# HGRN and forgetting-attention decays computed beside the first projection, one fewer matmul per attention score tile, and idle bf16 matmuls around the HGRN stage

## The reference

```python
# layer 0 of first_block
proj = x @ ev_w_in[e]
qa, fa, ia, ga, qb, kb, vb, fb = split_cols(proj, [HALF] * 7 + [FOX_HEADS])
ya = hgrn2(qa, fa, ia, ga, lb_all[layer], ev_hgrn_norm_g[e])
yb = forgetting_attention(qb, kb, vb, fb, ev_fox_bf[e])
mix = jnp.concatenate([ya, yb], axis=-1) @ ev_w_out[e]
# hgrn2: 4 heads of 128; lb = softmax-cumsum of a small table
log_f = jnp.log(lb + (1.0 - lb) * jax.nn.sigmoid(z))
k = (1.0 - lb) * jax.nn.sigmoid(-z)
b = cumsum(log_f)                    # the decay exponent, over time
# scores from q*exp(b), k*exp(-b), state passed from block to block, rms norm over 128, gate
# forgetting_attention: 8 heads of 64
log_f = jax.nn.log_sigmoid(f_logit + b_f)
c = jnp.cumsum(log_f, axis=1)
logits = q @ k.T * scale + c[query] - c[key]     # then mask, softmax, @ v
```

## Time and profile before

| what | us |
|---|---|
| median of the three timed runs | 3848.94 |
| the profiled execution's own time | 3850.37 |
| its span | 3848.6 |
| TensorE busy in it | 3598.5 (94%) |
| VectorE, ScalarE, GpSimd busy | 1619.7, 1334.2, 552.4 |
| first projection, last matmul begins at | 178.12 |
| attention stage, first matmul begins at | 316.82 |

### The profile page before, as it was taken

One profiled execution on the slowest core, in us unless ns is written; L12 is line 12 of the kernel. 1 busy time (PEld: TensorE's weight loads), 2 busy tenths in 40 slices (PEclk: granted clock), 3 DMA queues, 4 the chain that ended last, 5 costly groups with the idle time before them and its releaser, 6 DMA issues. The chain is left out here.

```text
span 3848.6 us, 42102 instructions
## 1 busy us (share of the span) xinstructions
PE 3598.5 (94%) x15648; PEld 2825.8 (73%) x15662; DVE 1619.7 (42%) x2091; ACT 1334.2 (35%) x1864; POOL 552.4 (14%) x446
## 2 busy tenths in 40 slices
PE   8878999998889999899998889999999999789998
PEld 7675668886666888688885468887788875578885
DVE  2284443335554333433345743335333235743335
ACT  3232232224553222433232543324333233533324
POOL 0030121101022110221000012202221000022202
PEclk9985899999999999999999899999999999899999
DMA  4200123322112332233220023322233220123322
GB/s 136 81 1 1 44 71 98 107 85 67 49 44 77 98 107 79 77 94 108 82 91 34 13 83 96 106 97 75 90 96 108 84 79 28 33 82 94 109 81 72
DMA packets 77745, 294.18 MB, mean 76 GB/s; under 512 B 8624, under 2 KB 11184, under 8 KB 77360
## 3 DMA queue, kind: packets, MB, share of 16 engines
q1 hardware_dynamic: 77616, 292.45, 23.9%
HBM read 290.32 MB, written 2.10 MB: 76 GB/s over the span
## 5 line engine op out<-in xcount | busy, mean ns | idle before, releaser
L146 DVE TENSOR_TENSOR w_low<-w_raw,w_high 128x1024 fp32r<-128x1024 f32 (+4 forms) x513 | 672.7, 1311 | 1578.5 <-ACT w_high L141 1578.5
L180 PE MATMUL bank<-x_high,w_high 128*128 128x512 f32 x2856 | 1130.4, 396 | 74.5 <-POOL x_low L224 22.0
L181 PE MATMUL bank<-x_low,w_high 128*128 128x512 f32 x2856 | 1120.4, 392 | 0.0
L182 PE MATMUL bank<-x_high,w_low 128*128 128x512 f32 x2856 | 1120.3, 392 | 0.0
L141 ACT CAST w_high<-w_raw 128x1024 fp32r<-128x1024 f32 (+4 forms) x513 | 555.0, 1082 | 872.8 <-PE bank L182 867.1
L180 PEld LDWEIGHTS bank<-x_high,w_high 128*128 128x128 f32 x2856 | 541.0, 189 | 206.4 <-issue 38.2
L182 PEld LDWEIGHTS bank<-x_high,w_low 128*128 128x128 f32 x2856 | 541.1, 189 | 113.3
L181 PEld LDWEIGHTS bank<-x_low,w_high 128*128 128x128 f32 x2856 | 541.9, 190 | 112.0 <-issue 2.1
L182 PE MATMUL bank<-hidden_high,w_low 128*128 128x512 f32 x1056 | 411.4, 390 | 0.0
L180 PE MATMUL bank<-hidden_high,w_high 128*128 128x512 f32 x1056 | 411.4, 390 | 0.0
L181 PE MATMUL bank<-hidden_low,w_high 128*128 128x512 f32 x1056 | 411.4, 390 | 0.0
(11 more groups left out here) (481 smaller groups left out, 3799.9 us busy)
## 6 DMA issues: line engine op xcount, KB each, us to landing
w_raw<-in_stream SPq DMA_DIRECT2D x381, 512.0 KB, 3.5
w_raw<-in_stream SPq DMA_DIRECT2D x96, 704.0 KB, 4.0
w_raw<-in_stream SPq DMA_DIRECT2D x16, 384.0 KB, 3.1
dft_positions<-in_dft SPq DMA_DIRECT2D x2, 2048.0 KB, 7.4
w_raw<-in_stream SPq DMA_DIRECT2D x4, 576.0 KB, 3.7
h<-in_x SPq DMA_DIRECT2D x8, 256.0 KB, 6.0
w_raw<-in_stream SPq DMA_DIRECT2D x16, 128.0 KB, 2.1
out<-result SPq DMA_DIRECT2D x4, 512.0 KB, 2.6
```

What stands on the lines that cost most here:

```text
L146: self.nc.vector.tensor_tensor(self.lo[:, j % 2, 0:size], self.raw[:, j % RAW_SLOTS, 0:size], self.hi[:, j % 2, 0:size].bitcast(F32), ALU. ...
L180: nc.tensor.matmul(out, lhs[0], rhs[0], start=start, stop=False)
L181: nc.tensor.matmul(out, lhs[0], rhs[1], start=False, stop=False)
L182: return nc.tensor.matmul(out, lhs[1], rhs[0], start=False, stop=stop)
```

## The change

- A new class `DecaySide` takes over the whole preparation of the HGRN stage, the constants and the forgetting-attention decays, cut into pieces that `linear_block` calls behind given jobs of the first projection. `constants_stage` and `fox_decay_stage` are gone, and with them two barriers. The transfer of the level masks moves from the HGRN stage to the head of the projection's DMA list.
- The eight-row steps of the attention decay stand behind jobs 21 to 26, the 16 scans behind jobs 16 to 19, the small table behind jobs 0 to 2, the constants behind job 3, the affine steps behind jobs 8 and 13.
- c is kept in one tensor `fox_c_parts` of 72 rows (high part in rows 0 to 7, low part in 64 to 71, zeros between), so that one matmul with `ident_fox` adds both. It now comes first in a unit, then the mask, then q by k.
- TensorE gets 14 idle bf16 matmuls at the end of the first projection, 8 between the last head's output and its variance, and 24 behind that variance.

```diff
@@ linear_block, after all jobs
+            if side:
+                side.end_pe(nc, C, pe, S)
@@ hgrn_stage, TensorE
-                pe.wait_ge(S.dve_step, 2 + 2 + 5 + HALF_T)
...
                     mm.then_inc(S.o_done, 1)
+                keep_warm(nc, C, C.bank[0], 8)
                 variance(HALF_T - 1)
+                keep_warm(nc, C, C.bank[0], 24)
@@ new
+class DecaySide:
+    NEGATED, PLUS, LOGS, SCAN, FOX = 7, 12, 14, 16, 21
...
+    def on_sync(self, nc, C, sp, S):
+        sp.dma_start(self.masks[:, :, :], C.level_dram).then_inc(S.masks_in, 16)
...
+    def end_pe(self, nc, C, pe, S):
+        pe.wait_ge(S.masks_in, 16)
+        pe.wait_ge(S.set, 9)
+        pe.wait_ge(S.evacuated, 4 + 21)
+        keep_warm(nc, C, C.bank[0], 14)
+
+    def on_act(self, nc, C, act, S, j):
...
+        if j == self.NEGATED:
+            act.wait_ge(S.evacuated, 4 + 8)
+            nc.scalar.activation(self.kk[:, :, :], prj[:, 4:8, :], ACT.Sigmoid,
+                                 scale=-1.0).then_inc(S.negated, 1)
+        if j == self.PLUS:
+            act.wait_ge(S.negated, 1)
+            nc.scalar.activation(prj[:, 4:8, :], prj[:, 4:8, :], ACT.Sigmoid).then_inc(S.plus, 1)
+        if j == self.LOGS:
+            act.wait_ge(S.f_ready, HALF_T)
+            nc.scalar.activation(prj[:, 4:8, :], prj[:, 4:8, :], ACT.Ln).then_inc(S.logs_ready, 1)
...
+    def on_dve(self, nc, C, dve, S, j):
...
+        if self.SCAN <= j < self.SCAN + HALF_T:
+            dve.wait_ge(S.logs_ready, 1)
+            for c in range(NB):
...
@@ scores
-                nc.tensor.matmul(bank[:, 0:keys], prj[r, 12 + t, qb * P:(qb + 1) * P],
-                                 prj[r, 16 + t, 0:keys], start=True, stop=False)
-                for part in (c_hi, c_lo):
-                    nc.tensor.matmul(bank[:, 0:keys], C.pick(h), part[:, 0:keys], start=False, stop=False)
-                return nc.tensor.matmul(bank[:, qb * P:keys], C.ident_bf, C.mask_after,
-                                        start=False, stop=True)
+            nc.tensor.matmul(bank[:, 0:keys], C.pick_fox(h), c_parts[:, 0:keys], start=True, stop=False)
+            nc.tensor.matmul(bank[:, qb * P:keys], C.ident_bf, C.mask_after, start=False, stop=False)
+            return nc.tensor.matmul(bank[:, 0:keys], prj[r, 12 + t, qb * P:(qb + 1) * P],
+                                    prj[r, 16 + t, 0:keys], start=False, stop=True)
```

More of the change, by code:

```diff
@@ L1397, in _, with hgrn_stage @@
                                                 ALU.mult).then_inc(S.normed, 1)
-def hgrn_stage(nc, C, prj, kk, va):
+def hgrn_stage(nc, C, prj, kk, va, masks):
     with ExitStack() as ctx:
@@ L1432, in hgrn_stage @@
         NL = LEVELS + 2
-        with stage(nc, "fetched act_step dve_step lb_in lb_exp f_ready logs_ready b_ready diff_ready decay_ready "
-                       "k_ready q_ready level_done masked_ready level_used turned copied state_done "
+        with stage(nc, "diff_ready decay_ready k_ready q_ready level_done masked_ready level_used turned copied state_done "
                        "state_ready o_done squared var logged rstd_ready y_ready") as S, nc.Block() as block:
-            @block.sync
-            def _(sp):
-                sp.dma_start(masks[:, :, :], C.level_dram).then_inc(S.fetched, 16)
             @block.scalar
             def _(act):
[L1443 to L1450, removed]
                 def square(h):
@@ L1512, in _ @@
             def _(dve):
[L1513 to L1548, removed]
                 def take_diff(h, i):
@@ L1721, in _ @@
             nc.vector.tensor_scalar(f, f, C.par("fox_bf")[0:HEADS, :], None, ALU.add).then_inc(S.biased, 1)
+        if j == self.FOX + 3:
             dve.wait_ge(S.logd, 1)
-            nc.vector.scalar_tensor_tensor(c, f, 0.0, work[0:HEADS, 0, :], ALU.min,
-                                           ALU.subtract).then_inc(S.low, 1)
+            nc.vector.scalar_tensor_tensor(c, f, 0.0, self.w[:, 0, :], ALU.min, ALU.subtract).then_inc(S.low, 1)
             dve.wait_ge(S.low, 1)
@@ L1727, in _ @@
             dve.wait_ge(S.low, 2)
[L1728 to L1757 removed]
+            nc.vector.tensor_tensor_scan(c, C.ones_row, c, 0.0, ALU.mult, ALU.add).then_inc(S.summed, 1)
+        if j == self.FOX + 5:
+            dve.wait_ge(S.fox_high, 1)
+            nc.vector.tensor_tensor(self.c_parts[64:72, :], c, self.c_parts[0:HEADS, :].bitcast(F32),
+                                    ALU.subtract).then_inc(S.fox_low, 1)
 def even_layer(nc, C):
@@ L1776, in even_layer @@
[L1776 to L1792 removed]
+        kk = sb("hgrn_k", [P, HALF_T, T])
@@ new lines, in even_layer @@
+        c_parts = ctx.enter_context(sbuf(nc, "fox_c_parts", [72, T], F32R))
+        masks = sb("level_masks", [P, LEVELS, P])
+        with ExitStack() as work:
+            linear_stage(nc, C, [feature(8, to_tiles(nc, prj), "act"),
+                                 feature(4, to_tiles(nc, prj, 8, 1, 1.0, ACT.Silu), "act"),
+                                 feature(4, to_tiles(nc, prj, 12, 1, HD ** -0.5), "act"),
+                                 feature(5, to_tiles(nc, prj, 16), "act"),
+                                 token(4, to_token_rows(nc, va), "dve", 2, T),
+                                 token(4, to_token_rows(nc, vb), "dve", 2, T)],
+                         source=Input("plain", C.h, DT, arrivals=C.x_in),
+                         side=DecaySide(nc, ctx, work, prj, kk, masks, c_parts))
@@ new lines, in even_layer, with scores @@
+        hgrn_stage(nc, C, prj, kk, va, masks)
+        def scores(pe, bank, h, qb, keys):
+            r, t = slice(HD * (h % 2), HD * (h % 2) + HD), h // 2
+            nc.tensor.matmul(bank[:, 0:keys], C.pick_fox(h), c_parts[:, 0:keys], start=True, stop=False)
+            nc.tensor.matmul(bank[:, qb * P:keys], C.ident_bf, C.mask_after, start=False, stop=False)
+            return nc.tensor.matmul(bank[:, 0:keys], prj[r, 12 + t, qb * P:(qb + 1) * P],
+                                    prj[r, 16 + t, 0:keys], start=False, stop=True)
```

133 lines of the change are left out of this document (81 added, 52 removed).

## The result

The changed kernel takes 3796.8 us, the median of four runs (3788.4 to 3807.1), beside 3850.7 before: a ratio of 0.9866, with an interval of 0.9824 to 0.9907. A second set of six runs, beside other runs of before, gave 0.9872 (0.9853 to 0.9892). So it is faster by 1.3%, about 50 us. The forecast of 3812 was 15 us too high, and the time lies inside the stated range of 3778 to 3830. The profiled execution took 3807.05 us of its own time, 43.3 less than the 3850.37 of before; the forecast's sum had been 37.3.

The account below looks back on a forecast made before the run. Bounds: a VectorE and ScalarE chain at the HGRN head, all engines' exchange in its heads, TensorE at 0.50 in attention. 18.3 − 2.3 + 7.0 + 12.3 + 2.0 = 37.3 us less than 3850.4, corrected to 3812; range 3778 to 3830.

Parts of the forecast that it names:

- Head of the HGRN stage, 18.3: Between projection and head 0's first difference: barriers, constants and chain removed, the difference starting at 182.5, 18.3 us gained.
- the waits, 2.3: In the projection: TensorE waits 0.75 us three times, in front of jobs 9, 14 and 16, 2.3 us lost.
- HGRN end and decay stage, 7.0: Between HGRN heads and attention: decay stage gone, variance at the high clock, attention starting at 309.8, 7.0 us gained.
- One matmul fewer, 12.3: In the 32 attention units: the removed low-part matmul saves 0.34 to 0.56 us each at the low clock, 12.3 in all.
- High clock at the start, 2.0: At the attention's start: TensorE at the high level for the first few us only, 2.0 us gained.
- If the clock rises where it does now: In the attention: the 12.3 us term assumed the clock rises behind the third block's closing transposes, at 414 in the old profile.
- A: In the attention: the clock comes back one block earlier, behind the second block, 15.3 us more gained, 3797; chance 0.25.
- B: In the attention: the clock stays high all through the stage, 34.3 us more gained, 3778; chance 0.12.
- C: Clock does not rise before the attention's end, or falls already at the variance: 3824, or 3832 with slow idle matmuls; chance 0.12.
- D: In the projection: the removed chain returns as waits, the masks' transfer costs 1 us, with C: about 3840; chance 0.06.
- E: In the projection behind job 7: a wait drops the clock to 0.50 and it stays; 3877 if for 12 jobs; chance 0.04.

Follow-up runs that it names:

- side_alone: The changed kernel with only the move of the decay work: idle matmuls taken out, attention units in their old form; ratio 0.9917 to the kernel before.
- best_two: The changed kernel with sums padded to 128 rows, idle matmuls in attention (two per 128-key unit, one per 256-key), at its end and in output projections; ratio 0.9832.

## Why the prediction came out as it did

**Head of the HGRN stage, 18.3, and the waits, 2.3: right.** The projection's last copies begin 182.48 − 178.54 = 3.9 later. 2.0 of that are the three waits, of 0.7 at most. The matmuls also start 0.15 later, and the clock rises for the first time at 19.4 instead of 18.1; the rest is not traced. The idle matmuls end at 185.5 and the difference follows 0.98 later (forecast 0.9). In all 14.3 us earlier, where the forecast had 16.0; side_alone shows the 14 idle matmuls' share: there the difference starts 3.50 us behind the beginning of the copies, in after 3.98. TensorE waits for no scan.

**HGRN end and decay stage, 7.0: right.** The variance ran at the high clock, the idle matmuls outlasted VectorE by 1.0 (1.3 forecast), and the attention's first matmul is 23.5 us earlier (23 forecast). From the last output matmuls to the attention's first it is 9.48 us instead of 17.19, 7.7 less (7.0 forecast). That the total fits as well as it does has a part of luck: the first difference came 1.7 us later than forecast, and the head loop and end, which I had left as they were, took 1.8 us less from that difference to VectorE's last product (291.51 − 186.46 against 307.66 − 200.80).

**One matmul fewer, 12.3: the size nearly, the reason not.** The units are shorter by 0.40, 0.40 and 0.51 (forecast 0.34, 0.34, 0.45), and by 0.36 at the high clock, some 13 us in 32 units. But the matmul gives 0.21 only. I had read its cost from its start to the next one's, and those 0.34 us are 0.13 more, about the 0.14 that the way from 8 rows to 128 costs. I priced the order at nothing, and it costs 0.19; I priced the rows at nothing, by full matmuls of the projection, and they give 0.38. The first two errors made the term too large and the third made it too small, so that its size came out nearly right was luck.

**High clock at the start, 2.0: right.** It lasted 2.6 us in one profile and 2.8 in the other, worth up to 1.9.

**"If the clock rises where it does now": this step failed.** The prediction tied the rise to the transposes that close a block, the third's in the forecast and the second's in A. It was not behind the third block in any of the profiles with 72 rows. Rival A (3797) named another place, behind the second block, and gave the rows as its ground; one of after's two profiles has the rise there, the other in the third block. I had set it at 0.25, because in before's trace the second block's closing had not brought the clock back. But that trace had the 8-row matmuls, the thing that the change takes away. In the first profile of after the stage is 19.6 us shorter against 14.3 forecast, in the second 32.1 (A's sum is 29.6). In the first profile that makes 5.3 of the 6.0 us by which the execution beat the sum. The runs near 3788 were not profiled, so that the rise also explains 3812 against 3797 is likely but not shown. That the measured 3796.8 is A's very number is in part luck, since after's rises lie 47 and 74 us into the stage. The range held because A and B were inside it. What decides where the clock comes back stays open. B did not happen, though idle matmuls at the right place make it happen, and best_two's stage of 73.6 us is near B's (121.2 − 14.3 − 34.3 = 72.6). Against after they give 15 us and not 34, since after had already come out 15 us below the forecast. C, D and E did not come; the projection stayed at 1.00 behind job 7 but for a stretch of 3.4 us at 159.3, which before had at 154.6.

## What to carry over

Read a matmul's price from kernels or rows where the neighbours differ too: a start-to-start distance holds the gap that the neighbour's row count makes, and padding a thin matmul to the full rows can give more than dropping one. Where a stage is bound by TensorE at 0.50, treat the place of the rise as the largest term, and ask which rows of before still hold once the thing that the change removes is gone. And try a few idle matmuls inside the shortest low units before placing any ahead of the stage: the 32 ahead were worth nothing that could be measured here, those inside 10 to 15 us by the ratios.

## What the runs showed of the hardware

- Between matmuls of 128 rows, one of 8 rows and 128 columns costs 0.27 us more on its way in and 0.14 on its way out than one of 72, at the low clock, and a unit of 512 keys at the high clock is 0.28 longer (3.12 against 2.84). 72 and 128 rows cost the same (units of 1.80, 2.97 and 4.14 us with either).
- The granted clock can fall 2.6 us into a stage that begins 0.81 us behind full-rate matmuls, with TensorE busy 2.25 of 2.57 us, and stay at 0.50 while the profile calls the engine busy for 71.7 of 71.7.
- The same program in two executions has the clock back 74.3 and 47.2 us into a stage, and a part of such a difference is given back later in the run (12.5 us in the stage, 5.9 in the whole).
